# Split weight tiles placed 64 bytes past a multiple of 128 bytes, with the memory's split tiles

## What is computed

```python
def swiglu(h, w1, w3, w2):
    return (jax.nn.silu(h @ w1) * (h @ w3)) @ w2
...
    q = (h @ w_q).reshape(B, S, MEM_HEADS, MEM_HEAD_DIM)
    k, v = jnp.split(m @ w_kv, 2, axis=-1)
```

## Time and profile before

| | before |
|---|---|
| median of 3 runs | 2549.39 us (2547.61 to 2551.35) |
| the profiled execution, its own time | 2550.2 us |
| its span, first to last instruction | 2548.0 us |
| mean granted TensorE clock | 0.978 |
| TensorE matmul busy | 2452.7 us (96%) |
| VectorE busy | 1239.7 us (49%) |
| ScalarE busy | 902.3 us (35%) |

### The profile page before, as it was taken

One profiled execution on the slowest core, in us unless ns is written; L12 is line 12 of the kernel. 1 busy time (PEld: TensorE's weight loads), 2 busy tenths in 40 slices (PEclk: granted clock), 3 DMA queues, 4 the chain that ended last, 5 costly groups with the idle time before them and its releaser, 6 DMA issues.

```text
span 2548.0 us, 30473 instructions
## 1 busy us (share of the span) xinstructions
PE 2452.7 (96%) x12342; PEld 2046.3 (80%) x12342; DVE 1239.7 (49%) x1477; ACT 902.3 (35%) x1223; POOL 70.7 (3%) x80
## 2 busy tenths in 40 slices
PE   7989999999999999999999999999898999999998
PEld 6657888888899788888788888798767977788886
DVE  6677533366736543332444432556585523444423
ACT  3353333213354433331333321344454434333311
POOL 0210000000002000000000000000000000000000
PEclk9999999998999999999999999999898999999999
DMA  8125522373322122222222222221200421222221
GB/s 336 68 86 214 197 98 99 148 272 120 105 85 90 66 99 99 91 101 89 81 99 99 99 99 99 95 83 67 67 1 34 140 92 34 94 89 96 99 99 66
DMA packets 40407, 267.36 MB, mean 105 GB/s; under 512 B 4378, under 2 KB 5658, under 8 KB 9218
## 3 DMA queue, kind: packets, MB, share of 16 engines
q1 hardware_dynamic: 31248, 219.87, 24.0%
q0 software_dynamic: 5696, 40.37, 4.1%
q10 hardware_dynamic: 3378, 5.91, 0.8%
HBM read 263.90 MB, written 2.24 MB: 104 GB/s over the span
## 4 chain that ended last, share of the span: by engine, by line
PE 85%; DVE 8%; ACT 4%; issue 1%; DMA 1%; SPq 0%; DVEq 0%; ACTq 0%
PE bank L223 24%; PE bank L225 24%; PE bank L224 24%; DVE w_lo L210 1%; ACT w_hi L206 1%; DMA work<-stream 1%; PE bank L2201 1%; PE bank L326 1%; PE bank L2284 1%; PE bank L2296 1%; DVE work L450 1%; PE bank L254 1%; PE bank L255 1%; PE bank L260 1%; PE bank L1921 1%
## 5 line engine op out<-in xcount | busy, mean ns | idle before, releaser
L223 PE MATMUL bank<-h_hi,w_hi 128*128 128x512 f32 x1880 | 740.1, 394 | 7.7 <-DVE h_lo L565 2.6
L224 PE MATMUL bank<-h_lo,w_hi 128*128 128x512 f32 x1880 | 734.5, 391 | 0.0
L225 PE MATMUL bank<-h_hi,w_lo 128*128 128x512 f32 x1880 | 734.5, 391 | 0.0
L210 DVE TENSOR_TENSOR w_lo<-raw,w_hi 128x2048 fp32r<-128x2048 f32 x192 | 439.9, 2291 | 532.6 <-ACT w_hi L206 532.6
L206 ACT ACTIVATE w_hi<-raw 128x2048 fp32r<-128x2048 f32 x192 | 366.2, 1907 | 410.5 <-PE bank L225 401.7
L223 PEld LDWEIGHTS bank<-h_hi,w_hi 128*128 128x128 f32 x1880 | 354.7, 189 | 87.7 <-issue 8.5
L225 PEld LDWEIGHTS bank<-h_hi,w_lo 128*128 128x128 f32 x1880 | 354.6, 189 | 74.5
L224 PEld LDWEIGHTS bank<-h_lo,w_hi 128*128 128x128 f32 x1880 | 354.8, 189 | 73.1 <-issue 0.5
L225 PE MATMUL bank<-g_hi,w_lo 128*128 (+1 forms) x704 | 273.9, 389 | 0.0
L223 PE MATMUL bank<-g_hi,w_hi 128*128 (+1 forms) x704 | 273.9, 389 | 0.0
L224 PE MATMUL bank<-g_lo,w_hi 128*128 (+1 forms) x704 | 273.9, 389 | 0.0
(11 more groups left out here) (292 smaller groups left out, 2699.8 us busy)
## 6 DMA issues: line engine op xcount, KB each, us to landing
raw<-stream SPq DMA_DIRECT2D x192, 1024.0 KB, 4.8
work<-stream POOLq DMA_DIRECT2D x19, 1024.0 KB, 5.3
h_plain<-stream POOLq DMA_DIRECT2D x16, 1024.0 KB, 5.4
work<-stream SPq DMA_DIRECT2D x13, 1024.0 KB, 12.3
work<-mlstm_rows ACTq DMA_DIRECT2D x8, 512.0 KB, 5.0
x<-xT SPq DMA_DIRECT2D x1, 2048.0 KB, 9.6
outT<-work SPq DMA_DIRECT2D x8, 256.0 KB, 2.3
work<-mlstm_rows ACTq DMA_DIRECT2D x8, 192.0 KB
```

Source lines behind the costliest of these rows:

```text
L210: nc.vector.tensor_tensor(w_lo[:, slot(m), :], raw[:, slot(m), :], w_hi[:, slot(m), :], ALU.subtract).then_inc(lo_split, 1)
L223: nc.tensor.matmul(out, stationary[0], moving[0], start=first, stop=False)
L224: nc.tensor.matmul(out, stationary[0], moving[1], start=False, stop=False)
L225: return nc.tensor.matmul(out, stationary[1], moving[0], start=False, stop=last)
```

## The change

64 bytes are left free between raw and w_hi. w_hi, w_lo and what is placed behind them (par, tab, mod, mod1, cond, small, inv_rows) move up by 64 bytes; inv_rows now ends at 125312, so the work area stays where it was. mem_hi and mem_lo are placed 64 bytes lower in it. No instruction is added or removed, and no semaphore is touched.

```diff
         h_plain = place("h_plain", [P, 4, UNIT], offset=at[0] - 4 * UNIT * 4)
         raw = place("raw", [P, 2, UNIT])
+        at[0] += 64
         w_hi = place("w_hi", [P, 2, UNIT], F32R)
         w_lo = place("w_lo", [P, 2, UNIT], F32R)
...
-        mem_hi = place("mem_hi", [P, KC, N_MEM], F32R, offset=work_at + 19456 * 4)
-        mem_lo = place("mem_lo", [P, KC, N_MEM], F32R, offset=work_at + 21504 * 4)
+        mem_hi = place("mem_hi", [P, KC, N_MEM], F32R, offset=work_at + 19456 * 4 - 64)
+        mem_lo = place("mem_lo", [P, KC, N_MEM], F32R, offset=work_at + 21504 * 4 - 64)
```

## The result

The change makes the kernel slower: 2598.7 us (median of 4 runs, 2591.6 to 2598.9) against 2548.8 us (4 runs, 2547.6 to 2551.4), a ratio of 1.0189 with a 95% interval of 1.0172 to 1.0205. The forecast was 2549 us and at most 2577 us. One execution of the kernel before, measured beside the last experiment, took 2802.6 us at a mean granted clock of 0.826 and is left out of the ratio there.

The account below looks back on a forecast made before the run. TensorE, busy in 96% of the span, was taken as the bound, so the cost per matmul counts. All terms summed to 0 on a span of 2548.0 us; predicted 2549 us, the median being 2549.4, range 2440 to 2577 us.

Parts of the forecast that it names:

- the count of 9864 steps: All split matmuls on TensorE: 8136 of 512 columns and 1728 of 256, taking 2051 us of 2548.0 us.
- The terms for ScalarE and VectorE: ScalarE writing w_hi, VectorE reading raw and w_hi and writing w_lo: 0 claimed, upper bound 3 us, under TensorE's work.
- the small tables: Accesses to par, tab, mod, small and inv_rows, whose remainder changes: nothing to win or lose, 0.
- SyncE's loads and the waits: SyncE's loads land in raw, which does not move, and the change adds no wait: 0.
- The term for moving operands: TensorE streaming weights in `tokens`, weights and memory in the memory stage, from 64: 0, upper bound 13.3 ns each.
- TensorE loads stationary weights from an address at 64 ... I take 0: 8136 + 192 weight loads and 192 of the memory: a slightly longer load hides beside 512 columns, 0.
- Rival A: TensorE's moving and weight reads collide; separate starts give 10 ns back on 9480 matmuls, 95 us, 2454 us; chance 0.17.
- Rival C: Stationary operands off 128 stall the array: 13.3 ns on 8136 + 384 matmuls, 113 us, 2662 us; chance 0.08.
- Rival B: Moving fp32r operands off 128 need one more piece: 13.3 ns on 1728 matmuls, 23 us, 2572 us; chance 0.22.
- The 32 cycles "whatever its width": Each split matmul on TensorE takes 13.3 ns, 32 cycles, above its columns, at 512 and 256 alike.
- rival D: Nothing changes: reads go by units dividing 64 bytes, the excess belongs to fp32r itself; the forecast, chance 0.46.

Follow-up runs that it names:

- the last experiment: Against the kernel before, the 18 units whose weights move lie at 112 bytes, all others at 0: 2543.94 us against 2551.13, ratio 0.9977.

## Why the prediction was wrong

**What held.** What bounds the kernel, the method (the distance of starts, not the duration) and the count of 9864 steps held: the sum of those steps is 48.6 to 49.8 us for 49.9 measured; that the second agrees to 0.1 us is luck, with executions 7 us apart. The terms for ScalarE and VectorE (0; 1909 and 2292 ns), the small tables (0), SyncE's loads and the waits (0) held. The term for moving operands was taken as 0 and measured -3.6 us for `tokens` and -0.3 us for the memory.

**The step that failed** is "TensorE loads stationary weights from an address at 64 ... I take 0": 8136 times 6.6 ns, 53.7 us. Its row was a float32 load of tab at 96 that takes the 190 ns of one at 0. That row is right and doesn't answer the question: it is the duration of a load by itself beside a slow stream. What the change moved was the distance between the two operands of an fp32r matmul, and there is no row of this in the trace of before: all four kinds had distance 0 modulo 256. The working asked for the address of each operand alone, one by one. The run with all tiles moved together shows that this address costs nothing (226.5 ns with h and w both at 64).

**Rival A** had that distance in it and got a chance of 0.17, held down by two arguments. The first, that the two addresses drift through every relative position whatever the start, fell: 64 bytes of distance change the step by 6.6 ns. The second, that g lies 256 bytes off h's position without a change, was true and I read it wrongly: it speaks only for distances of whole 256 bytes, as the gap of 256 shows (ratio 0.9994). Had the distance been granted, the sign would still have been open: A expected 0 to be the collision, and for 512 columns no distance tried is quicker than 0. The memory's steps, which A left as they were because both operands went to 64 modulo 128, moved too: their distance became 128, and 119.2 ns came of 119.9.

**Rival C** had the right operand and the right sign, with a chance of 0.08 for the full size and 0.04 for a few cycles. Its size was double (13.3 ns for 6.6), its reason, one piece more per block because of the address, is wrong: with h and w both at 64 their steps lose nothing, and with w at 128 past h, a multiple of 128, nearly all is.

**Rival B** (2572 us) fell: moving operands at 64 became quicker, 117.8 for 120.0 ns.

**The 32 cycles "whatever its width"** hold at distance 0 for 256, 384 and 512 columns. As a property of fp32r itself, which rival D made of them, they don't: 256 columns run with 16 when the weights move at distance 112, 512 with 42 when hardly anything is loaded, and at half the clock there is no excess at all (426.7 ns). The rule that the prediction cited (the Trainium skill, TensorE: Matmul & The Clock Gate, "Wait — 56ns, not 53.3ns?": 215.7 ns for 512 columns) disagrees with every stretch of fp32r steps of 512 columns at the full clock in these runs; the lowest mean is 226.5 ns.

**What stays open.** That the cost of this change comes from the distance modulo 256 is shown: the steps follow it when h moves along and g stays, and 256 bytes cost nothing. It does not set the step alone: 16, 124 and 128 bytes each have two values. How it acts is not shown: why 256 bytes, why 120 and 240 are as quick as 0 where 112, 116, 124 and 128 are slow, why 16 allows two rhythms, why a full load at distance 0 makes the stream quicker than nearly none, why 112 bytes suit moving weights and not stationary ones, and why nothing of it is left at half the clock. Between 128 and 256 only 240 was tried; 144, which is what the quickest moving weights have from their own side, was not tried with 512 columns. Some distances were tried in mixers alone and others in feed-forwards alone. Why the granted clock differs by 0.002 between some kernels, which is worth 6 us, is open too. The kernel with 128 bytes is some 2 us quicker than its steps say.

## What to carry to other kernels

Where fp32r matmuls follow each other with a load beside each, look at where the moving and the stationary tile start relative to each other, modulo 256 bytes; here 0 was as good as any for 512 columns (226.7 ns, 230.0 to 234.4 at most others) and, where the weights move 256 wide, 112 was best of those tried (113.3 for 120.0), so tiles of both uses may want an offset of their own. Padding or a reordered placement that shifts one of them can cost 2% with no wait and no busy share to show for it; the distance of starts, averaged over some 50 steps at the full clock, shows it at once. And a nearest row only bounds a cost if it has the same pair of operands at the same rate: one operand's row says nothing about the pair.

## What was not expected of the hardware

- The fp32r step depends on the distance of two tiles modulo 256 bytes: for 512 columns 226.7 ns at 0, 120, 240 and 256, against 232.4 at 4, 230.7 at 8, 233.4 at 64, 234.4 at 96, 231.7 or 233.3 at 124 and 232.4 or 233.4 at 128.
- Which operand lies ahead matters: at 112 bytes and 256 columns 120.0 ns with the weights stationary, 113.3 with the weights moving.
- At half the clock (granted 0.50) the step is 426.7 ns at distance 0 and at 64, the columns alone.
- At 16 bytes it runs at 226.7 or at 233.2 ns, and what decides is not shown.
- Loading 4 columns for 128 does not shorten the step: 231.0 for 226.7 ns.
- In the changed kernel's rhythm of 233.3 ns single steps of 231 and 236 ns alternate; at the same distance, with all tiles moved together, they are 233 and 234 ns.
